# Gate products moved in among the second half of the first table's rows, one-hots by VectorE one token at a time

## The reference, cut to what matters

```
q = (t @ w_q).reshape(T, 8, 2, 128)
s1, s2 = q[:, :, 0] @ sk1.T, q[:, :, 1] @ sk2.T        # scores of 128 keys each
v1, i1 = top_k(s1, 16); v2, i2 = top_k(s2, 16)
cand = v1[..., :, None] + v2[..., None, :]             # 256 candidates a head
vc, ic = top_k(cand, 16)
expert = i1[ic // 16] * 128 + i2[ic % 16]              # 8 heads x 16 experts a token
gate = softmax(vc)
a = einsum(t, u_tab[expert]);  w = gate * gelu(a);  y = w @ v_tab[expert]
```

## Time and profile before

| | |
|---|---|
| median of 3 runs | 2430.15 us |
| the profiled execution | 2430.07 us, its span 2428.3 us |
| busy over the span | PE 2163.8, DVE 1458.9, ACT 1188.2, POOL 897.9 us |
| stages of layer 0, about | start to 117, mixer to 301, output projection and queries to 402, first table to 784, gate stage to 906, second table to 1269 us |
| stages of layer 1, about | mixer to 1456, first table from 1556 to 1938, gate stage to 2060, second table to 2413 us |

### The profile page before, as it was taken

The page is one execution under the profiler, slowest core; times in us unless marked ns, Lnnn a source line. Parts: engine busy times, 40 slices in busy tenths (PEclk is TensorE's granted clock), DMA queues, the critical chain, the costliest instruction groups (busy, mean ns, idle before and its releaser), DMA issues.

```text
span 2428.3 us, 40340 instructions
## 1 busy us (share of the span) xinstructions
PE 2163.8 (89%) x13500; PEld 1953.7 (80%) x13500; DVE 1458.9 (60%) x2371; ACT 1188.2 (49%) x2096; POOL 897.9 (37%) x382
## 2 busy tenths in 40 slices
PE   5787789999999569999998877999999956999998
PEld 4776578999999558888877657899999955888886
DVE  7578427997001886677767842799700088555555
ACT  8521424555544764444442242455554476445543
POOL 0003025988888540000000302598988854000000
PEclk9698789999999999999999878999999999999999
DMA  7632043555555006777763203455555500555553
GB/s 263 236 104 87 27 135 128 184 180 187 179 182 181 15 0 243 254 264 261 266 226 115 87 27 113 131 182 180 183 181 182 182 18 0 173 193 195 190 193 110
DMA packets 103454, 378.56 MB, mean 156 GB/s; under 512 B 11488, under 2 KB 11872, under 8 KB 102880
## 3 DMA queue, kind: packets, MB, share of 16 engines
q1 hardware_dynamic: 102672, 373.74, 45.7%
q10 hardware_dynamic: 720, 4.00, 0.4%
HBM read 375.46 MB, written 2.23 MB: 156 GB/s over the span
## 4 chain that ended last, share of the span: by engine, by line
PE 41%; POOL 22%; issue 22%; DVE 10%; ACT 2%; DMA 2%; POOLq 1%; DVEq 0%; SPq 0%; ACTq 0%
PE bank L1591 29%; POOL split_lo L473 20%; PE bank L1569 3%; PE bank L1291 3%; POOL hots L484 3%; DMA ring<-stream 1%; DVE hots L1126 1%; PE bank L1254 1%; DVE hots L1124 1%; PE bank L1465 1%; DVE grid L832 1%; PE bank L1265 1%; PE bank L1316 1%; DVE grid L962 1%; ACT grid L646 1%
## 5 line engine op out<-in xcount | busy, mean ns | idle before, releaser
L473 POOL TENSOR_TENSOR split_lo<-ring,split_hi 128x1024 fp32r<-128x1024 f32 x296 | 728.8, 2486 | 245.8 <-ACT split_hi L673 245.5
L1502 PE MATMUL bank<-h_hi,split_hi 128*128 128x256 f32 x2304 | 657.0, 285 | 29.6 <-DVE h_lo L1068 21.3
L1503 PE MATMUL bank<-h_lo,split_hi 128*128 128x256 f32 x2304 | 654.7, 284 | 0.0
L1504 PE MATMUL bank<-h_hi,split_lo 128*128 128x256 f32 x2304 | 654.6, 284 | 0.0
L1502 PEld LDWEIGHTS bank<-h_hi,split_hi 128*128 128x128 f32 x2304 | 444.6, 193 | 34.0 <-issue 18.6
L1157 DVE TENSOR_TENSOR split_lo<-ring,split_hi 128x1024 fp32r<-128x1024 f32 x248 | 303.8, 1225 | 249.0 <-ACT w_hi L749 248.9
L1504 PEld LDWEIGHTS bank<-h_hi,split_lo 128*128 128x128 f32 x2304 | 445.1, 193 | 0.0
L1503 PEld LDWEIGHTS bank<-h_lo,split_hi 128*128 128x128 f32 x2304 | 445.0, 193 | 0.0
L748 ACT ACTIVATE split_hi<-ring 128x1024 fp32r<-128x1024 f32 x248 | 263.2, 1061 | 354.3 <-PE bank L1591 354.3
L673 ACT ACTIVATE split_hi<-ring 128x1024 fp32r<-128x1024 f32 x296 | 298.5, 1051 | 274.1 <-PE bank L1504 273.8
L1591 PE MATMUL bank<-split_hi,w_hi 128*128 128x512 f32 x1024 | 316.8, 390 | 0.0
(11 more groups left out here) (270 smaller groups left out, 2695.2 us busy)
## 6 DMA issues: line engine op xcount, KB each, us to landing
ring<-stream SPq DMA_DIRECT2D x658, 512.0 KB, 3.3
ada_ring<-stream SPq DMA_DIRECT2D x48, 512.0 KB, 4.2
spill<-tables ACTq DMA_DIRECT2D x1, 1152.0 KB, 5.5
tables<-spill ACTq DMA_DIRECT2D x1, 1152.0 KB, 7.5
xT<-x_in SPq DMA_DIRECT2D x1, 1024.0 KB, 10.1
s5raw<-s5w ACTq DMA_DIRECT2D x2, 512.0 KB, 5.3
y_out<-hT SPq DMA_DIRECT2D x1, 1024.0 KB, 3.9
KM<-mixc SPq DMA_DIRECT2D x1, 576.0 KB, 8.2
```

Of the source, the lines that this page charges most:

```text
L473: gp.tensor_tensor(split_lo[:, j, :], ring[:, (e0 + j) % RING, :], split_hi[:, j, :].bitcast(F32), ALU.subtract)\
L1502: mm(dst, hi, x_hi, start=start, stop=False, skip_group_check=not group)
L1503: mm(dst, hi, x_lo, start=False, stop=False, skip_group_check=not group)
L1504: return mm(dst, lo, x_hi, start=False, stop=stop, skip_group_check=not group)
```

## The change

- The first table keeps its first 64 rows as they were (turns 0 to 7). The other 64 rows (late rows, FIRST_LATE = 64) are taken in 32 steps: PE makes the gate products of 8 tokens (an octet) into two banks of 4 to 7, then a pair of rows, then the next octet.
- DVE multiplies the rows of grid that have their gelu by the octet's gates and copies the gates of the rows still to come into grid (weigh). The gelu of a late pair goes to a small tile, late_gelu, for the tokens whose gates are in grid already, and straight into grid for the others; weigh_late multiplies the first part in.
- All one-hots are made by DVE: 16 tensor_scalar operations an octet, each 128 x 128, with the token's column of pick as scalar operand. hotA's has two such operands (index and gate). There is one hots tile. ACT and POOL make none.
- The order on DVE in step p: wait for the products of p, weigh(p), one_hots(p + 1), wait for the gelu of pair p, weigh_late(p).
- Picks are turned after row 60 instead of 104, exponentials taken after 6 turns instead of 9.
- At line 1106 eight multiplications become one over 128 x 2048.
- In the mixer the imaginary part goes from POOL to DVE; the S5 input products come earlier in PE's order; DVE makes the first phase operations ahead of the norm; ACT makes sine and cosine ahead of one copy.
- The second table begins on w_done, after the last weigh_late and a memset of zeros, and no longer on w_ready.

More of the change, by code:

```diff
@@ L565, in _ @@
                     act.dma_start(tables[:, :], spill).then_inc(tables_in, 16)
+                nc.scalar.activation(dt5, small_of(l, "ldt"), ACT.Exp).then_inc(s5_exp, 1)
                 if l == 0:
@@ L588, in _ @@
                 nc.scalar.activation(cosT, tmp, ACT.Sin, scale=-TWOPI).then_inc(trig_ready, 1)
+                copy(l, "ik", ik)
+                act.wait_ge(s5_lr, l + 1)
+                nc.scalar.activation(mag5, lr5, ACT.Exp).then_inc(s5_mag, 1)
                 for i in range(2):
@@ L693, in _, with gelu_pair @@
                 first = KEYS // 2 * l
+                def gelu_pair(i, j):
+                    act.wait_ge(a_ready, i * 4 + (first + j + 1))
+                    for w in range(2):
+                        high(PQ + 2 * j + w + SPLIT, i, 8)
+                    nc.scalar.activation(grid[:, bass.ds(i * (8 * T) + j * 2 * T, 2 * T)], bank[:, j, :],
+                                         ACT.Gelu_apprx_tanh).then_inc(gelu_done, 1)
                 def gelus(i):
                     for j in range(4):
[L697 to L703, removed]
+                        gelu_pair(i, j)
+                with act.Fori(0, 6, 1) as i:
                     gelus(i)
@@ L707, in _ @@
                     nc.scalar.activation(vc[:, i, :, :], vc[:, i, :, :], ACT.Exp).then_inc(gate_exp, 1)
[L708 to L713, removed]
-                act.wait_ge(turned_picks, l + 1)
-                for i in range(TT):
-                    nc.scalar.activation(pick[:, :, i * P:i * P + P], bank[:, 6 + i, 0:3 * P].rearrange("p (r t) -> p r t", r=3),
-                                         ACT.Copy).then_inc(pick_ready, 1)
@@ L719, in _ @@
-                with act.Fori(14, 16, 1) as i:
-                    gelus(i)
-                def column_hots(n, j):
-                    for t in range(2, 8):
-                        last = nc.scalar.activation(hotB[j][:, t, :], iota, ACT.Abs, scale=-1.0, bias=pick[:, 1, bass.ds(n * 8 + t, 1)])
-                    last.then_inc(hot_step, 1)
-                    act.wait_ge(hot_step, n + (T // 8 * l + 1))
-                    nc.scalar.activation(hotB[j][:, 2:8, :], hotB[j][:, 2:8, :], ACT.Relu, scale=-1.0, bias=1.0).then_inc(column_ready, 1)
@@ L740, in _ @@
+                act.wait_ge(w_done, l + 1)
                 late = e0 + EARLY
```

121 lines of the change are left out of this document (38 added, 83 removed).

## The result

The changed kernel takes 2618.64 us (median of 4 runs, 2609.79 to 2619.53) against 2430.49 us for the kernel before on the same chip: ratio 1.077, 95% interval 1.0751 to 1.0789, so 188 us slower. The forecast was 2546 us, within 2365 to 2580 us.

The account below looks back on a forecast made before the run. PE was taken as never resting in the table's second half, followed by a 121 us gate stage a layer. 2430.07 us plus 119.7 for both late halves less 4 for the mixer gave 2546 us, range 2365 to 2580.

Parts of the forecast that it names:

- The break-in of POOL: Late half: DVE's one-hot chain doesn't keep POOL out; DVE gets one instruction in at each boundary of POOL's 2.4 us subtractions.
- Rival B: Late half: the chain of one-hots keeps POOL out, a step is about 9.0 us, 2401 us in all; chance 0.07.
- Rival C: One-hots with scalar operands don't use the interface shared with POOL, step 8.5 to 8.9 us, about 2380 us; chance 0.14.
- Rival A: One-hots at or under about 0.17 us all fit before POOL returns, step 8.5 us, 2369 us; chance 0.13.
- Rival D: Late half: a mild form where the two steps fall together at 9.4 us, no change, about 2430 us; chance 0.03.
- A pair of steps: Late half: two steps take 22.5 us, PE idling from 7.7 to 14.7; 16 pairs make 360 us a layer.
- The schedule by hand: Late half: hand timeline of PE, ACT, POOL and DVE over two steps, 22.4 us, taken as 22.5.
- The end: Behind the last row: copies, low parts and late product take 6.3 us until the second table's clearing matmul may start.
- The edit of line 1106 at nothing: One multiplication in place of eight costs nothing and saves DVE some 37 us ahead of the picks.
- The picks in time by 25 us: Picks, turned after row 60, are needed by about 588 and ready with about 25 us of slack.
- The mixer's -4 us: Mixer edits: -3.3 us in layer 0, -2.0 in layer 1, about 1 us given back; sum -4 us, bounds 0 and -14.
- The range: Its own range, from the one-hot's and the mixer's bounds, is 2515 to 2580 us; widened for fast rivals, 2365 to 2580.

Follow-up runs that it names:

- experiment 1: Changed kernel with POOL's low part in the table's second half covering 32 of a block's 1024 elements, the rest left out: 2360.21 us, ratio 0.972.
- experiment 5: Changed kernel with the low parts of the table's second half made by DVE in place of POOL: 2374.3 us, ratio 0.9765.
- experiment 6: Changed kernel with column one-hots made by ACT, only the 8 row one-hots by DVE, POOL's low parts kept: 2372.05 us, ratio 0.9749.
- experiment 8: Changed kernel with an octet's one-hots by three DVE instructions of 1024 elements in place of 16 of 128: 2413.77 us, ratio 0.992.
- Experiment 2: Changed kernel plus 48 unused matmuls that PE issues before waiting for the one-hots in every second step: 2553.01 us, ratio 1.0513.
- experiment 10: Kernel before with only line 1106 edited, one multiplication of 2048 in place of eight of 256: 2444.71 us, ratio 1.006.
- experiment 3: Changed kernel with the one multiplication of 2048 put back as eight of 256: 2628.12 us, ratio 1.0814.
- experiment 9: Kernel before with only the mixer's edits (block order, place of norm and exponentials, imaginary part on DVE): 2431.05 us, ratio 0.9998.

## Why the prediction was right, and where it fell short

The difference between the two profiled executions is 189.0 us, of which 115.7 were forecast. The rest is 30.4 us in the first table and its gates in each layer (21 in the late half, 7.3 ahead of it, 2.1 in the clearing), 7.6 us in the mixers, 4.8 us in the second table of layer 0.

- **The break-in of POOL** (right). "While POOL has work DVE gets one in at each of POOL's boundaries": experiments 1, 5, 6 and 8 each take away one side of it and win 205 to 258 us. Rival B falls, POOL breaks in at 701.31. Rival C falls, one-hots wait 2.5 us. Rival A falls: a one-hot is 0.20 us with one scalar operand and 0.26 with two, 0.23 as a mean, against the 0.22 taken. That all would fit if they were short enough is borne out from the other side by experiment 6, where eight of 0.26 us fit into POOL's 2.66 us of rest. Rival D falls with the time.
- **A pair of steps** (mechanism right, size wrong: the failed step). The forecast had PE at its full pace after the wait: "PE idled from 7.7 to 14.7; then gates and rows, to 22.4". It took every PE duration from stretches in which PE had not stood still. A hint stood in the earlier trace rows: in the gate stage, where PE is busy 57% of the time, the clock was 0.94 and 0.96, not 1.00. The price stood in the trace of the kernel before as well: behind an idle time of 8.95 us the gate products of 16 tokens took 6.01 us, where 8 tokens take 2.05:

```profile
792.75 6.01 PE L1569 MATMUL bank<-hots 128*128 128x128 f32 x32 [8.95 <-POOL hots L484]
```

Measured with the clock kept, the pair is 21.8 us; with the fall to the low clock it is 24.0. Experiment 2 sizes this term: 66 us over both layers. It stands against 73 us missing, but the two are not the same sum. The schedule by hand was 0.6 us a pair too long (the wait was taken as 7.0 us and is 6.3 to 6.7, PE's step as 7.7 us and is 7.6): with the clock kept a late half is 355.7 us, not 366.3. These 21 us over both layers hide most of 31 us of other errors: line 1106, the clearing, the mixers and the second table of layer 0, below.
- **The end** (right but for the clock). 6.3 us to the clearing matmul, measured 6.4 us of idle time; the clearing itself then takes 5.83 us instead of 3.70, the low clock again, 2 us a layer.
- **The edit of line 1106 at nothing** (wrong). It was costed by DVE's slack alone, which is the wrong side: the question was who waits for DVE's instruction, not what DVE waits for. Price: about 7 us a layer in the rows, shown by experiment 10 as +12.6 us. The prediction's own rows had it: an instruction of 2.3 us on DVE is to POOL what POOL's 2.4 us are to DVE.
- **The picks in time by 25 us** (right). The changed kernel shows no wait at their turn: in layer 0 DVE has the last of them at 566.5, and PE turns them at 593.9, 27 us later. DVE's part was done at 550.6 (forecast 552), the exponentials came at 563.8 (forecast near 555). With eight multiplications the picks are 10.7 us late, not the 5 of the forecast (experiment 3).
- **The first octet** (overlooked). The one-hots are wanted right behind row 63, and the first octet of them stands beside POOL as well: four of its sixteen wait for a subtraction, and PE idles 3.7 us. The clock falls behind this shorter wait too: the gates take 3.78 us.
- **The mixer's -4 us** (zero, experiment 9). The stall ahead of the second S5 product came, 11.24 us for the forecast 8.8, in part because DVE waits 15.94 us for the exponential that was moved behind two sines and a copy on ACT, a wait that the forecast did not follow up; the gain behind it is eaten by that. PE no longer waits for DVE at the place of line 1380, but it gets there at 239.35 in layer 0, by its own work, where 233.5 was forecast and the kernel before is at 236.79. The profiled changed kernel's 3.8 us more in layer 1 and 4.8 us in the second table of layer 0 are not the edits' doing: experiment 3, with the same mixer, shows 1.9 us and 0.4 us there. What they are stays open.
- **The range.** The lower end of the forecast's own range doesn't follow from its bounds, 12 us for the one-hots and 10 for the mixer: 2524 us, not 2515.

## What to carry to other kernels

Before moving work into a stage because an engine is free there, list what else that engine's instructions exclude, and count instructions beside the other's, in both directions: many short ones in a chain pay per boundary of a long neighbour, and one long one makes the neighbour late. Find the moment at which the neighbour returns, for the cost is a threshold there: POOL's hold cost this kernel 258 us with three or four one-hots of every second octet behind its return, 12 us with half as many one-hots, and 54 with three wide instructions. And when a forecast leaves TensorE idle again and again, price the matmuls behind each gap at the clock that rows behind such a gap show, not at the stage's mean.

## What the runs showed of the hardware

- After 6.2 to 6.7 us without a matmul the granted clock was 0.50 for the next 4.2 to 5.5 us, 30 times in this kernel; issuing 48 matmuls of no use in each gap made it 66 us faster.
- DVE and POOL exclude each other by whole instructions in both directions: a one-hot of 0.26 us takes 2.50 us behind a subtraction of 2.4, and a subtraction takes 3.1 us on average beside a chain of DVE's 2.3 us instructions. That is the rule of the Trainium skill, SBUF — State Buffer, Who interferes with whom, which the prediction weighed, and the traces agree.
- A tensor_scalar of 128 elements with a column of scalars each: the next one starts 0.20 us later with one such operand and a comparison, 0.26 with two operands and two operations. Both wait for POOL like those with constants.
- DVE reducing 2048 elements (2.29 us each time) kept its undisturbed length beside POOL, while a multiplication of 2048 beside it took 4.38 and a comparison 4.41 us where 2.29 is undisturbed. The same section of the skill says that tensor_reduce never contends; the trace agrees.
- A pattern that alternates between two steps can end on either foot: with pairs of 23.9 and 24.0 us the last row came 5.8 and 6.5 us later in the kernel in which the waits fell on the other octets (experiment 3).
